# Modulation sums of block 1 placed earlier on VectorE, and a semaphore of its own for the second mixer's weights

## The chip, the cores and the metric

One NeuronCore of a Trainium2 chip runs the whole program in one launch. The metric is the device time of an execution in microseconds (us); less is better.

## What is computed

Two blocks of a transformer for one sequence of 256 tokens of width 1024, all in float32. The part that matters here is the start of block 1:

```python
mod = jax.nn.silu(c) @ ada_w[l] + ada_b[l]
sh_m, sc_m, g_m, sh_f, sc_f, g_f = jnp.split(mod, 6, axis=-1)
h = modulate(rms_norm(x, mix_norm_w[l]), sh_m, sc_m)
proj = h @ w_in[l]
y_r = rwkv7_group(proj[..., :RWKV_COLS], ...)
y_m = mlstm_group(proj[..., RWKV_COLS:], ...)
y = jnp.concatenate([y_r, y_m], axis=-1) @ w_out[l]
x = x + g_m[:, None, :] * y
```

`mod` is six vectors of 1024, each a product of `silu(c)` with a 1024x1024 piece of `ada_w`. The first two (shift and scale of the first norm) are needed before `proj`; the other four only after both mixers have begun. `proj` has 3336 columns: 13 chunks of 256 and eight gate columns. After block 1 come its mixture of experts and a second model of two layers with their own modulation, attention and MLPs.

## The kernel before

The program is written for the five engines by hand; semaphores order them. What it does in the first 200 us:

**The stream of weights.** SyncE (`block.sync`, L822 on) issues one list of 1 MB loads through a ring of eight buffers of 8 KB per partition. The list (L438 to 444) is `ada` 0 to 7, then in turn `win 7, ada 8, win 8, ada 9, win 9, ada 10, win 10, ada 11, win 11, ada 12, win 12, ada 13, win 0, ada 14, win 1, ada 15, ...`, `win 6, ada 20`, and last `ada` 21 to 23. Place i of the list goes to buffer i % 8, and its issue waits until place i - 8 has been used: a `win` chunk by TensorE, an `ada` piece by VectorE (`v_ada`). SyncE issues strictly in the order of the list. So `ada 14` (place 21) waits for the use of `ada 10` (place 13) and stands in the queue behind `win 0` (place 20).

**The modulation sums.** `ada_slot(n)` (L1560) on VectorE waits until piece n has landed and adds two products of 128x1024 to one of three sums (L1570 for the first product of a vector, L1572 for the others). Four pieces make a vector; where a piece opens the fourth, fifth or sixth vector (n = 12, 16, 20), it first waits for `t_ada`, TensorE's use of the sum that had been in the same place. VectorE takes its instructions strictly in the program's order: what stands behind an `ada_slot` that waits for its load, waits too.

**The chunks of `proj`.** `columns(n)` on TensorE makes 32 matmuls with chunk `win n` (L2245 or L2247). The order is 7, 8, the eight gate columns (`w.if`, L2261) and a small product for the attention bias of the second model (L2265), then 9, 10; transposes and broadcasts of the gate rows (`m.bc`, L2273 and L2275, behind `m.rows` of VectorE), `scores` 0 and 1 (L2252); chunk 11; then a wait for `m.z` of VectorE, `scores` 2 and 3, chunks 12 and 0; a wait for `m.pt` and the product of the second mixer (L2294, L2297); chunks 1 to 5, two of the modulation vectors (L2309, L600), chunk 6.

**The second mixer (mLSTM) on VectorE.** In order: gate bias (`w.gb`, L1612), the convolution (`m.conv`, L1630 and L1633), gate rows (`m.lf` of ScalarE awaited; L1639 to L1644), multiplication by the sigmoid of ScalarE (L1646; with it `m.rows` is reached), `m.z` (L1650 to L1654, behind `m.bc` of TensorE), `m.pt` (L1662 to L1666), and later the token shifts of the first mixer (`shift(n)`, L1619 and L1621). Between them stand the `ada_slot` calls.

**The bias write.** ScalarE sends, behind the gate rows, the attention bias of the second model to DRAM (L1316): 8 partitions are read 128 times each, 1.5 MB in rows of 1536 bytes, on ScalarE's own DMA queue (q10 in the profile; SyncE's is q1, GpSimd's q0).

**The small loads.** GpSimd issues them (L895 to L925). `gate_in` counts seven: two pieces of the gate columns, two gate biases, and the three small matrices `rwkv_w_up`, `rwkv_a_up` and `rwkv_g_up` of the first mixer. `hot_in` counts the two for the attention bias. VectorE (L1611) and TensorE (L2258) wait for all seven of `gate_in`; TensorE waits for `hot_in` ahead of L2265.

Of the kernel before, what the change touches and what calls it, by code (L numbers as in the profile page):

```python
# [114 lines left out]
def program(nc, A, out):  # L115
    ctx = ExitStack()
    with ctx:
        def sb(name, shape, dt=F32):
            return ctx.enter_context(nc.sbuf_tensor(name, shape, dt))

        def sem(name):
            return ctx.enter_context(nc.semaphore(name))
# [22 lines left out]
        def area(kb, words):  # L145
            return arena[:, int(kb * KB):int(kb * KB) + words]

        def area_r(kb, words):
# [49 lines left out]
        wup = sb("wup", [P, 2, 512])  # L198
        gup = area(47, 512)
# [13 lines left out]
        x_in, c_in, prm_in, col_in, par_in, gate_in, row_in = (  # L213
            sem(n) for n in ("x_in", "c_in", "prm_in", "col_in", "par_in", "gate_in", "row_in"))
# [94 lines left out]
        hots = arena[0:64, 30 * KB:30 * KB + 384]  # L309
        rel_sb = arena[0:64, 32 * KB:32 * KB + 8]  # L310
# [34 lines left out]
            sem(n) for n in ("t_gv", "a_gv", "t_gather", "t_gu", "t_turn", "t_dn", "t_scatter", "t_fin", "a_hg", "a_silu", "a_y", "v_sel", "v_act",  # L345
                             "v_hg", "v_turn", "v_ye", "v_ada2", "v_fin"))
        ring2 = [sem(f"ring2_{i}") for i in range(RING)]
        t_bin, t_bout, hot_in = (sem(n) for n in ("t_bin", "t_bout", "hot_in"))
        mlp_in = ring2
        ring2_n = [16 * len(range(i, 13, RING)) for i in range(RING)]  # L350
        t_up, t_ft, t_fd, a_fact, a_ft, v_fact_t, a_w1, v_w1, a_w2, v_w2 = (
# [100 lines left out]
        def loaded(eng, key):  # L452
            eng.wait_ge(ring_in[place[key] % RING], 16 * (place[key] // RING + 1))

        def slot(key):
            return ring[:, place[key] % RING, :]
# [411 lines left out]
        def _(pool):  # L868
# [46 lines left out]
            pool.dma_start(w_if[:, :, 32:36], w_in_t[:, :, 3332:3336]).then_inc(gate_in, 16)  # L915
            pool.dma_start(gate_b[0:4, 0:1], A["mlstm_i_b"].rearrange("o h -> h o")).then_inc(gate_in, 16)
            pool.dma_start(gate_b[32:36, 0:1], A["mlstm_f_b"].rearrange("o h -> h o")).then_inc(gate_in, 16)
            pool.dma_start(rel_sb[0:32, :], A["rel_bias_2"]).then_inc(hot_in, 16)
            pool.dma_start(hots[0:33, :], A["hots"]).then_inc(hot_in, 16)
            pool.wait_ge(v_ada, 16)  # L920
            pool.dma_start(wup[0:64, 0, :], A["rwkv_w_up"][0]).then_inc(gate_in, 16)
            pool.dma_start(wup[64:128, 1, :], A["rwkv_a_up"][0]).then_inc(gate_in, 16)
            pool.dma_start(gup[:, :], A["rwkv_g_up"][0]).then_inc(gate_in, 16)
            pool.dma_start(gate1[:, 0, :], A["ada_b"][:, 2 * D:3 * D].to_broadcast([P, D])).then_inc(par_in, 16)
            pool.dma_start(gate1[:, 1, :], A["ada_b"][:, 5 * D:6 * D].to_broadcast([P, D])).then_inc(par_in, 16)  # L925
            c = Counter(pool, g["c"], STEP["c.zeros"])
# [632 lines left out]
        def _(dve):  # L1559
            def ada_slot(n):  # L1560
                vec, q = n // 4, n % 4
                loaded(dve, ("ada", n))
                w = slot(("ada", n)).rearrange("p (t n) -> p t n", t=2)
                acc = macc[:, vec % 3, :]
                if q == 0 and vec >= 3:
                    dve.wait_ge(t_ada, vec - 2)
                for r in range(2):
                    k = 2 * q + r
                    if k == 0:
                        ins = nc.vector.tensor_scalar(acc, w[:, r, :], ccol[:, k:k + 1], None, ALU.mult)  # L1570
                    else:
                        ins = nc.vector.scalar_tensor_tensor(acc, w[:, r, :], ccol[:, k:k + 1], acc, ALU.mult, ALU.add)  # L1572
                    ada.link(ins)
# [30 lines left out]
            v_norm(dve, "n", mod_c[:, 0, :], mod_c[:, 1, :], mod_mix, meanwhile=lambda: ada_slot(6))  # L1604


            c = Counter(dve, v["w"])
            dve.wait_ge(t["w"], STEP["w.prm"])
            c.link(nc.vector.tensor_copy(prm_c[:, :], ps[:, 0, 256:408]))
            c.at("w.prmc")  # L1610
            dve.wait_ge(gate_in, 16 * 7)  # L1611
            c.link(nc.vector.tensor_scalar(gate_b[:, 1:2], gate_b[:, 0:1], 1 / CAP, None, ALU.mult))  # L1612
            c.at("w.gb")
            c.at("w.pre")
# [1 line left out]
            def shift(n):  # L1616
                dve.wait_ge(a["w"], STEP[f"w.col{n}"])
                dt = dtmp[:, :].rearrange("p (i t) -> p i t", i=2)
                c.link(nc.vector.tensor_tensor(dt, raw[:, n % 2, :, 0:256], raw[:, n % 2, :, 1:257], ALU.subtract))  # L1619
                for i in range(2):  # L1620
                    c.link(nc.vector.scalar_tensor_tensor(u[:, 2 * n + i, :], dt[:, i, :], mu_c[:, 2 * n + i:2 * n + i + 1],  # L1621
                                                          raw[:, n % 2, i, 1:257], ALU.mult, ALU.add))


            cm = Counter(dve, v["m"])
            ada_slot(8)
            ada_slot(9)
            for i in range(4):
                dve.wait_ge(a["w"], STEP[f"w.col{7 + i // 2}"])
                cm.link(nc.vector.tensor_scalar(qk[:, i, :], convraw[:, i, 3:259], cw_c[:, 12 + i:13 + i], cb_c[:, i:i + 1],  # L1630
# [3 lines left out]
                                                           cw_c[:, 4 * j + i:4 * j + i + 1], qk[:, i, :], ALU.mult, ALU.add))  # L1634
            cm.at("m.conv")

            dve.wait_ge(a["m"], STEP["m.lf"])
            one4 = ones2[0:4, :]
            cm.link(nc.vector.tensor_scalar(mrow[0:4, 0, :], mrow[0:4, 0, :], CAP, None, ALU.mult))  # L1639
# [2 lines left out]
            cm.link(nc.vector.tensor_tensor_scan(mrow[0:4, 5, :], one4, mrow[0:4, 4, :], 0.0, ALU.mult, ALU.max))  # L1642
            cm.link(nc.vector.tensor_tensor(mrow[32:36, 4, :], mrow[0:4, 2, :], mrow[0:4, 5, :], ALU.subtract))
            cm.link(nc.vector.tensor_copy(sel4[:, :, :], ident[0:4, 0:4].unsqueeze(2).to_broadcast([4, 4, P])))  # L1644
            dve.wait_ge(a["m"], STEP["m.sig"])
            cm.link(nc.vector.tensor_tensor(qk[:, :, :], qk[:, :, :], qsig[:, :, :], ALU.mult))  # L1646
            cm.at("m.rows")
            ada_slot(10)
            dve.wait_ge(t["m"], STEP["m.bc"])
            cm.link(nc.vector.tensor_copy(mcol[:, :, :], ps[:, 0, 0:128].rearrange("p (a n) -> p a n", a=2)))  # L1650
            for h in range(4):
# [2 lines left out]
                cm.link(nc.vector.tensor_scalar(mz[:, h, 256:384], mb[:, 128:256], mcol[:, 1, h:h + 1], 0.0,  # L1654
                                                ALU.subtract, ALU.max))
            cm.at("m.z")
            ada_slot(11)
            ada_slot(12)
            dve.wait_ge(a["m"], STEP["m.exp"])
            dve.wait_ge(g["c"], STEP["c.masks"])  # L1660
            cmask = m_causal.unsqueeze(1).to_broadcast([P, 4, P])
# [4 lines left out]
                cm.link(nc.vector.scalar_tensor_tensor(mz[:, h, :], ps[:, sc_bank[h], 0:384], 0.125, mz[:, h, :],  # L1666
                                                       ALU.mult, ALU.mult))
            cm.at("m.pt")
            ada_slot(13)
            ada_slot(14)  # L1670
            shift(0)
            dve.wait_ge(t["m"], STEP["m.num"])
            den, rec = small[:, 16:24], small[:, 24:32]
# [13 lines left out]
                                                AX_X, ALU.add))  # L1687
            cm.link(nc.vector.tensor_scalar(small[:, 8:16], small[:, 8:16], 1 / P, EPS, ALU.mult, ALU.add))
            cm.at("m.ss")
            ada_slot(15)  # L1690
            dve.wait_ge(g["m"], STEP["m.rs"])
            for tt in range(TT):
                yv = ym[:, tt, :].rearrange("p (h n) -> p h n", h=4)
# [2 lines left out]
            cm.at("m.s")  # L1696
            for n in range(1, 7):
                shift(n)
                ada_slot(15 + n)
            c.at("w.shift")  # L1700

            dve.wait_ge(t["w"], STEP["w.if"])
# [516 lines left out]
        def _(pe):  # L2219
# [15 lines left out]
            def columns(n):  # L2235
                i = win_order.index(n)
                loaded(pe, ("win", n))
                if i >= 2:
                    pe.wait_ge(a["w"], STEP[f"w.col{win_order[i - 2]}"])
                w = slot(("win", n)).rearrange("p (t n) -> p t n", t=8)  # L2240
                for j in range(2):
                    o = ps[:, 6 + i % 2, 256 * j:256 * j + 256]
                    for k in range(KT):
                        if n < 9:
                            ins = nc.tensor.matmul(o, w[:, k, P * j:P * j + P], hT[:, k, :], start=k == 0, stop=k == KT - 1)  # L2245
                        else:
                            ins = nc.tensor.matmul(o, hT[:, k, P * j:P * j + P], w[:, k, :], start=k == 0, stop=k == KT - 1)  # L2247
                ins.then_inc(t_win, 1)
# [6 lines left out]

            for n in (7, 8):
                columns(n)
            pe.wait_ge(gate_in, 16 * 7)  # L2258
            pe.wait_ge(v["w"], STEP["w.prmc"])
            for k in range(KT):  # L2260
                ins = nc.tensor.matmul(ps[0:36, 0, 0:256], w_if[:, k, :], hT[:, k, :], start=k == 0, stop=k == KT - 1)  # L2261
            c.mark(ins)
            c.at("w.if")
            pe.wait_ge(hot_in, 32)
            nc.tensor.matmul(ps[0:SWA_H, 4, 0:384], rel_sb[0:33, :], hots[0:33, :], start=True, stop=True).then_inc(t_bias, 1)  # L2265

            for n in (9, 10):
# [69 lines left out]

            c = Counter(pe, t["r"])
            pe.wait_ge(a["r"], STEP["r.u"])
            for tt in range(TT):  # L2340
                nc.tensor.matmul(ps[:, 4 + tt, :], u[:, 13, P * tt:P * tt + P], gup[:, :], start=True, stop=True)
            pe.wait_ge(v["r"], STEP["r.sq"])
# [299 lines left out]
            for i, (kind, _) in enumerate(ITEMS):  # L2642
                ahead = i < NI - 1 and "over" in (kind, ITEMS[i + 1][0])
                both_next = i % 2 and i < NI - 1
                if i == 0 or "over" not in (kind, ITEMS[i - 1][0]):
                    gate_up(i, 0)
                    gate_up(i, 1)
                if i:
                    scatter(i - 1)
                if both_next:  # L2650
                    gather(i // 2 + 1, 0)
                turn(i)
                if both_next:
                    gather(i // 2 + 1, 1)
                if i == 0:
                    gv_columns(3, ps[:, 5, 0:8])
                    gv_columns(4, ps[:, 5, 8:16]).then_inc(t_fin, 1)
                    for h in range(2):
                        gv_gate(2, h, h)
                    for h in range(2):  # L2660
                        gv_gate(5, h, 2 + h)
                if ahead:
                    gate_up(i + 1, 0)
                down(i)
                if ahead:
                    gate_up(i + 1, 1)
# [96 lines left out]
            for j in range(6):  # L2763
                hs = range(4 * j, 4 * j + 4) if j < 2 else range(2 * (j - 2), 2 * (j - 2) + 2)
                n = P if j < 2 else 2 * P
# [9 lines left out]
            for j in range(6):  # L2775
# [3 lines left out]
                for i in range(4):  # L2779
                    n = 4 * j + i  # L2780
# [100 lines left out]
```

## Time and profile before

| | us |
|---|---|
| median of 3 runs | 1256.24 |
| lowest and highest | 1245.6, 1258.23 |
| the profiled execution, its own time | 1254.31 |
| its span in the trace | 1252.6 |
| TensorE busy in the span | 1070.0 (85%) |
| VectorE busy | 640.0 (51%) |
| ScalarE busy | 351.5 (28%) |
| mean granted TensorE clock | 0.922 |

Times inside the trace count from the start of the span; the execution's own time is 1.7 us longer. A row of the timeline has the start, the duration, the engine, the line, the operation with what it writes and reads, how many stand in the row, and in square brackets the idle time before it and who ended it. SPq and ACTq are the instructions by which SyncE and ScalarE issue DMAs. "PEclk" is the granted clock of TensorE: 1.00 is 2.4 GHz, 0.50 is 1.2 GHz.

### The profile page before, as it was taken

The numbers are of one execution on the slowest core, as the hardware profiler recorded it, in microseconds if no ns is written. First come the engines' busy times: TensorE is split into PE (matmuls) and PEld (weight loads), VectorE is DVE, ScalarE is ACT, GpSimd is POOL, SyncE is SP. The second block draws the span as 40 slices with busy tenths as digits, with TensorE's granted clock in tenths as the row PEclk, the third lists the DMA queues.
The fourth block names the chain that finished last, engine by engine and source line by source line (L and its number), as shares of the span: only waits on it lengthen the run. The fifth ranks groups of instructions, "written<-read, shape, count | busy, mean of one in ns | idle before, by whom it ended". The sixth has DMA issues, their size and how long they took to land.

```text
span 1252.6 us, 16197 instructions
## 1 busy us (share of the span) xinstructions
PE 1070.0 (85%) x6588; PEld 814.6 (65%) x6588; DVE 640.0 (51%) x812; ACT 351.5 (28%) x440; POOL 178.0 (14%) x234
## 2 busy tenths in 40 slices
PE   1898977999978899999539794979999976999995
PEld 1787844997535455555227683858888865888884
DVE  6565567646444333323045727376757467553433
ACT  1130024241111111111023105166354315543531
POOL 4701013000200133231011004011111130000000
PEclk9998987999977999999869997889999977999998
DMA  9979638204679999999979703056676461545510
GB/s 352 351 163 307 242 123 305 102 1 169 228 305 408 383 401 353 356 339 355 407 226 371 277 1 135 1 203 251 235 294 225 134 247 73 192 144 194 225 67 34
DMA packets 114090, 287.48 MB, mean 230 GB/s; under 512 B 16406, under 2 KB 42334, under 8 KB 114026
## 3 DMA queue, kind: packets, MB, share of 16 engines
q1 hardware_dynamic: 94514, 245.45, 52.6%
q10 hardware_dynamic: 7560, 26.74, 6.3%
q0 software_dynamic: 11952, 14.38, 3.8%
q8 instruction: 46, 0.75, 0.2%
q14 instruction: 18, 0.15, 0.0%
HBM read 334.23 MB, written 2.62 MB: 269 GB/s over the span
## 4 chain that ended last, share of the span: by engine, by line
PE 68%; DMA 13%; DVE 10%; SPq 3%; ACT 2%; issue 2%; POOL 1%; DVEq 0%; ACTq 0%; POOLq 0%
PE ps L573 29%; PE ps L2245 6%; PE ps L2582 5%; DMA arena<-in_moe_w_down_dram 4%; PE ps L2561 4%; PE ps L2421 3%; DMA macc<-in_ada_w_dram 3%; PE ps L2609 3%; DMA ring<-in_w_in_dram 2%; PE ps L2508 2%; PE ps L2687 2%; SPq L763 1%; PE ps L2624 1%; DMA ring<-in_ada_w_dram 1%; SPq L619 1%
## 5 line engine op out<-in xcount | busy, mean ns | idle before, releaser
L578 DVE TENSOR_TENSOR ring_parts<-ring,arena_parts 128x2048 fp32r<-128x2048 f32 x65 | 146.6, 2286 | 49.1 <-ACT arena_parts L1109 42.1
L573 PE MATMUL ps<-arena_parts,macc_parts 128*128 128x512 f32 x512 | 166.0, 396 | 0.0
L573 PE MATMUL ps<-arena_parts,gate_parts 128*128 128x512 f32 x288 | 114.6, 398 | 8.3 <-DVE hT_parts L578 8.3
L573 PE MATMUL ps<-ring_parts,gate_parts 128*128 128x512 f32 x288 | 113.5, 394 | 0.0
L573 PE MATMUL ps<-arena_parts,hT_parts 128*128 128x512 f32 x288 | 113.4, 394 | 0.0
L573 PEld LDWEIGHTS ps<-arena_parts,macc_parts 128*128 128x128 f32 x512 | 96.2, 188 | 19.6
L573 PE MATMUL ps<-ring_parts,macc_parts 128*128 128x512 f32 x256 | 99.8, 390 | 0.0
L1109 ACT CAST arena_parts<-ring 128x2048 fp32r<-128x2048 f32 x32 | 60.3, 1908 | 84.5 <-DMA ring<-in_mlp_w_dram 43.4
L2245 PE MATMUL ps<-hT,ring 128*128 128x256 f32 x288 | 70.1, 409 | 5.6 <-DMA ring<-in_w_in_dram 5.6
L2245 PEld LDWEIGHTS ps<-hT,ring 128*128 128x128 f32 x288 | 59.5, 208 | 15.3 <-DMA ring<-in_w_in_dram 6.0
L573 PEld LDWEIGHTS ps<-arena_parts,gate_parts 128*128 128x128 f32 x288 | 55.1, 191 | 20.5 <-DVE hT_parts L578 9.1
L2582 PE MATMUL ps<-ring,hT 128*32 128x256 f32 x1024 | 61.7, 387 | 5.3 <-issue 3.4
L466 POOL TENSOR_TENSOR small<-small,nhalf 128x1 f32<-128x1 f32 x16 | 10.0, 625 | 390.1 <-DVE small L500 390.0
L573 PEld LDWEIGHTS ps<-arena_parts,hT_parts 128*128 128x128 f32 x288 | 55.0, 191 | 11.7
L573 PEld LDWEIGHTS ps<-ring_parts,gate_parts 128*128 128x128 f32 x288 | 55.1, 191 | 11.3
L1089 ACT CAST arena_parts<-ring 128x2048 fp32r<-128x2048 f32 x32 | 60.0, 1911 | 5.3 <-DMA ring<-in_mlp_w_dram 5.2
L578 DVE TENSOR_TENSOR macc_parts<-ps,macc_parts 128x512 fp32r<-128x512 f32 x32 | 22.1, 691 | 75.9 <-ACT macc_parts L1133 75.9
L2012 DVE SCALAR_TENSOR_TENSOR macc_parts<-ps,small,macc_parts 128x512 fp32r<-128x512 f32 x24 | 16.9, 747 | 85.8 <-ACT macc_parts L1439 85.8
L1572 DVE SCALAR_TENSOR_TENSOR macc<-ring,ccol,macc 128x1024 f32<-128x1024 f32 x42 | 54.0, 1285 | 8.5 <-DMA ring<-in_ada_w_dram 7.1
L2582 PEld LDWEIGHTS ps<-ring,hT 128*32 128x32 f32 x1024 | 34.3, 112 | 33.9 <-issue 13.5
L2609 PE MATMUL ps<-arena,gate 128*32 128x512 f32 x384 | 45.6, 607 | 10.8 <-DMA arena<-in_moe_w_down_dram 9.5
L573 PEld LDWEIGHTS ps<-ring_parts,macc_parts 128*128 128x128 f32 x256 | 48.2, 188 | 9.3
(539 smaller groups left out, 1799.0 us busy)
## 6 DMA issues: line engine op xcount, KB each, us to landing
ring<-in_mlp_w_dram SPq DMA_DIRECT2D x40, 1024.0 KB, 7.6
arena<-in_moe_w_down_dram SPq DMA_DIRECT2D x16, 2048.0 KB, 12.4
ring<-in_ada_w_dram SPq DMA_DIRECT2D x29, 1024.0 KB, 13.4
ring<-in_mlp_w_dram ACTq DMA_DIRECT2D x24, 1024.0 KB, 7.1
ring<-in_moe_w_up_dram SPq DMA_DIRECT2D x10, 2048.0 KB, 22.3
ring<-in_moe_w_gate_dram SPq DMA_DIRECT2D x10, 2048.0 KB, 17.8
arena<-in_ada_w_dram SPq DMA_DIRECT2D x15, 1024.0 KB, 7.0
ring<-in_w_in_dram SPq DMA_DIRECT2D x13, 1024.0 KB, 18.4
```

The source lines that it names most:

```text
L573: ins = nc.tensor.matmul(o, l, r, start=start and i == 0, stop=stop and i == 2, skip_group_check=True)
L578: return eng.tensor_tensor(lo, x, hi.bitcast(F32), ALU.subtract)
L1089: nc.scalar.copy(mlp_hi[s_], ring[:, s_, :]).then_inc(a_w2, 1)
L1109: nc.scalar.copy(mlp_hi[s_], ring[:, s_, :]).then_inc(a_w1, 1)
L1572: ins = nc.vector.scalar_tensor_tensor(acc, w[:, r, :], ccol[:, k:k + 1], acc, ALU.mult, ALU.add)
L2245: ins = nc.tensor.matmul(o, w[:, k, P * j:P * j + P], hT[:, k, :], start=k == 0, stop=k == KT - 1)
L2421: ins = nc.tensor.matmul(o, lhs[:, gi, hh], rhs[:, gi, hh], start=True, stop=True)
L2508: ins = nc.tensor.matmul(ps[:, 4 + j, :], hT[:, k, P * (j // 2):P * (j // 2) + P], w, start=k == 0, stop=k == KT - 1)
L2561: ins = nc.tensor.matmul(ps[:, 6 + i // 2, 256 * (i % 2):256 * (i % 2) + 256], xn[:, tt, P * k:P * k + P], picked[:, tt, :], start=tt == 0 ...
L2582: ins = nc.tensor.matmul(ps[rows, 4 + i % 2, FE * half:FE * half + FE], hT[:, k, P * (i % 2) + CAPQ * j:P * (i % 2) + CAPQ * j + CAPQ], w[ ...
L2609: ins = nc.tensor.matmul(ps[rows, 6 + h, :], tb[:, P * f + CAPQ * j:P * f + CAPQ * j + CAPQ], down_w[:, j, f, 512 * h:512 * h + 512], star ...
L2687: ins = nc.tensor.matmul(o, w[:, k, P * j:P * j + P], hT[:, k, :], start=k == 0, stop=k == KT - 1)
```

## The change

The calls of `ada_slot` move forward on VectorE, past the waits and past the mixer's work. The table shows what stands ahead of each step. No piece is added or dropped.

| ahead of | before | after |
|---|---|---|
| the copy of the parameters (L1609) | | 8, 9 |
| the convolution | 8, 9 | 10, 11 |
| the wait for `m.lf` | | 12 |
| the wait for `m.sig` | | 13 |
| the wait for `m.bc` (ahead of `m.z`) | 10 | 14 |
| the wait for `m.exp` (ahead of `m.pt`) | 11, 12 | 15 |
| `shift(0)` | 13, 14 | 16 |
| the wait for `m.rs` | 15 | 17 |
| behind `shift(1)` to `shift(6)` | 16 to 21, one each | 18 to 21, one each behind `shift(1)` to `shift(4)` |

The two loads of the attention bias now count on `gate_in` and the three small matrices on a semaphore of their own, `lora_in`; so `gate_in` is awaited at six. TensorE waits for `lora_in` ahead of the product with `gup` (L2341) and no longer for `hot_in`.

```diff
-            pool.dma_start(rel_sb[0:32, :], A["rel_bias_2"]).then_inc(hot_in, 16)
-            pool.dma_start(hots[0:33, :], A["hots"]).then_inc(hot_in, 16)
+            pool.dma_start(rel_sb[0:32, :], A["rel_bias_2"]).then_inc(gate_in, 16)
+            pool.dma_start(hots[0:33, :], A["hots"]).then_inc(gate_in, 16)
             pool.wait_ge(v_ada, 16)
-            pool.dma_start(wup[0:64, 0, :], A["rwkv_w_up"][0]).then_inc(gate_in, 16)
-            pool.dma_start(wup[64:128, 1, :], A["rwkv_a_up"][0]).then_inc(gate_in, 16)
-            pool.dma_start(gup[:, :], A["rwkv_g_up"][0]).then_inc(gate_in, 16)
+            pool.dma_start(wup[0:64, 0, :], A["rwkv_w_up"][0]).then_inc(lora_in, 16)
+            pool.dma_start(wup[64:128, 1, :], A["rwkv_a_up"][0]).then_inc(lora_in, 16)
+            pool.dma_start(gup[:, :], A["rwkv_g_up"][0]).then_inc(lora_in, 16)
...
+            ada_slot(8)
+            ada_slot(9)
             c = Counter(dve, v["w"])
             dve.wait_ge(t["w"], STEP["w.prm"])
             c.link(nc.vector.tensor_copy(prm_c[:, :], ps[:, 0, 256:408]))
             c.at("w.prmc")
-            dve.wait_ge(gate_in, 16 * 7)
+            dve.wait_ge(gate_in, 16 * 6)
...
             cm = Counter(dve, v["m"])
-            ada_slot(8)
-            ada_slot(9)
+            ada_slot(10)
+            ada_slot(11)
...
             cm.at("m.conv")
 
+            ada_slot(12)
             dve.wait_ge(a["m"], STEP["m.lf"])
...
+            ada_slot(13)
             dve.wait_ge(a["m"], STEP["m.sig"])
             cm.link(nc.vector.tensor_tensor(qk[:, :, :], qk[:, :, :], qsig[:, :, :], ALU.mult))
             cm.at("m.rows")
-            ada_slot(10)
+            ada_slot(14)
             dve.wait_ge(t["m"], STEP["m.bc"])
...
             cm.at("m.z")
-            ada_slot(11)
-            ada_slot(12)
+            ada_slot(15)
             dve.wait_ge(a["m"], STEP["m.exp"])
...
             cm.at("m.pt")
-            ada_slot(13)
-            ada_slot(14)
+            ada_slot(16)
             shift(0)
...
             cm.at("m.ss")
-            ada_slot(15)
+            ada_slot(17)
             dve.wait_ge(g["m"], STEP["m.rs"])
...
             for n in range(1, 7):
                 shift(n)
-                ada_slot(15 + n)
+                if n < 5:
+                    ada_slot(17 + n)
             c.at("w.shift")
...
-            pe.wait_ge(gate_in, 16 * 7)
+            pe.wait_ge(gate_in, 16 * 6)
...
-            pe.wait_ge(hot_in, 32)
...
             pe.wait_ge(a["r"], STEP["r.u"])
+            pe.wait_ge(lora_in, 16 * 3)
```

## Rows read from the trace of the kernel before

**Rows 1.** The page, part 4: shares of the chain that ended last, by engine

```profile
PE 68%; DMA 13%; DVE 10%; SPq 3%; ACT 2%; issue 2%; POOL 1%; DVEq 0%; ACTq 0%; POOLq 0%
```

**Rows 2.** The chain that ended last, in order of time: start us, us, what

```profile
68.67 30.57 DMA ring<-in_w_in_dram
99.28 9.43 PE ps L2245 x32
...
113.97 34.64 PE ps L2245 x160
148.61 1.72 PE ps L2309 x4
```

**Rows 3.** Timeline of TensorE, 38 to 240 us

```profile
75.48 0.33 PE L2273 MATMUL ps<-ident,arena 64*128 64x64 f32 x2
...
85.62 0.71 PE L2252 MATMUL ps<-arena 64*128 64x256 f32 x4
...
86.48 7.17 PE L2247 MATMUL ps<-ring,hT 128*128 128x256 f32 x32
99.28 9.43 PE L2245 MATMUL ps<-hT,ring 128*128 128x256 f32 x32 [5.62 <-DMA ring<-in_w_in_dram]
```

**Rows 4.** Busy time by engine in the stretch 99 to 102 us, then clock, DMA

```profile
99.00:102.00 3.00, 2.72 (x6) 2.18 (x7) 0.29 (x1) 0.00 (x0) 0.00 (x0) 0.50 1.00 350
```

**Rows 5.** Timeline of VectorE, 30 to 110 us and behind 110 us

```profile
49.34 0.15 DVE L1612 TENSOR_SCALAR gate_b<-gate_b 36x1 f32<-36x1 f32 x1 [8.08 <-DMA arena<-in_rwkv_g_up_dram]
...
54.39 0.41 DVE L1630 TENSOR_SCALAR arena<-arena,prm_c 128x256 f32<-128x256 f32 x1
...
60.87 1.53 DVE L1633 SCALAR_TENSOR_TENSOR arena<-arena,prm_c 128x256 f32<-128x256 f32 x3
65.53 0.28 DVE L1639 TENSOR_SCALAR arena<-arena 4x256 f32<-4x256 f32 x1 [3.14 <-ACT arena L1311]
...
68.17 0.41 DVE L1644 COPY arena<-ident 4x512 f32<-4x512 f32 x1
71.74 1.23 DVE L1646 TENSOR_TENSOR arena<-arena 128x1024 f32<-128x1024 f32 x1 [3.15 <-ACT arena L1321]
...
77.84 0.29 DVE L1650 COPY arena<-ps 128x128 f32<-128x128 f32 x1 [2.23 <-PE ps L2275]
...
81.40 0.35 DVE L1654 TENSOR_SCALAR arena<-ps,arena 128x128 f32<-128x128 f32 x1
...
101.71 2.61 DVE L1572 SCALAR_TENSOR_TENSOR macc<-ring,ccol,macc 128x1024 f32<-128x1024 f32 x2 [5.77 <-DMA ring<-in_ada_w_dram]
...
169.40 2.61 DVE L1572 SCALAR_TENSOR_TENSOR macc<-ring,ccol,macc 128x1024 f32<-128x1024 f32 x2
```

**Rows 6.** Timeline of SyncE's DMA issues, 0 to 240 us (`ada 11`, `ada 14`, `win 1`)

```profile
36.90 8.13 SPq L838 DMA_DIRECT2D ring<-in_ada_w_dram  x1
...
75.63 0.37 SPq L838 DMA_DIRECT2D ring<-in_ada_w_dram  x1
76.04 7.53 SPq L841 DMA_DIRECT2D ring<-in_w_in_dram  x1
```

**Rows 7.** Line L838, the one issue at 36.9 us (`ada 11`)

```profile
DMA to landing us min/median/max: 21.4/21.4/21.4
```

**Rows 8.** Line L838, the one issue at 75.6 us (`ada 14`)

```profile
DMA to landing us min/median/max: 26.0/26.0/26.0
```

**Rows 9.** Timeline of ScalarE: the issue of the bias write

```profile
65.96 1.28 ACTq L1316 DMA_DIRECT2D bias_rows<-arena  x1
```

**Rows 10.** DMA queues, 68 to 70 us: packets, MB, share of 16 engines

```profile
q10 hardware_dynamic: 70, 0.11, 45.4%
q1 hardware_dynamic: 8, 0.02, 3.0%
```

**Rows 11.** DMA queues, 88 to 98 us

```profile
q10 hardware_dynamic: 326, 0.50, 41.8%
q1 hardware_dynamic: 334, 0.34, 9.6%
```

More of the change, by code:

```diff
@@ L347, in program @@
         ring2 = [sem(f"ring2_{i}") for i in range(RING)]
-        t_bin, t_bout, hot_in = (sem(n) for n in ("t_bin", "t_bout", "hot_in"))
+        t_bin, t_bout, lora_in = (sem(n) for n in ("t_bin", "t_bout", "lora_in"))
         mlp_in = ring2
```

## The prediction

> **What bounds the kernel now.** I read the page first: its chain of work that ended last is 68% TensorE, 13% DMA and 10% VectorE [rows 1]. So an edit on VectorE counts only where TensorE waits for VectorE, or where it moves a load. I then read that chain in order of time for the first 200 us, where all edits lie [rows 2]. TensorE works through the chunks of `proj` without a pause up to 93.65 us (86.48 + 7.17, [rows 3]); then it stands 5.62 us for chunk `win 0`, whose load took 30.57 us. After that nothing holds it until it has finished its first modulation vector behind chunk 5: chunk 0 from 99.28, the product of the second mixer, chunks 1 to 5 in 34.64 us, that is 6.93 us a chunk. Chunk 0 itself took 9.43 us. The granted clock at its start was 0.50, 1.2 GHz, after the pause [rows 4]; the pause has cost 9.43 - 6.93 = 2.5 us in clock besides its 5.62.
>
> Why did `win 0` need 30.57 us? The views of the queues and the timelines say it. ScalarE issues the bias write at 65.96 [rows 9]. From then on its queue q10 holds some 45% of the 16 engines, as many as eight of them busy nearly all the time [rows 10]. At 68 to 70 us SyncE's queue q1 is almost empty (8 packets): everything issued ahead of `win 0`, so `ada 13` too, is through. And late in the write, from 88 to 98 us, q1 gets 334 packets of about 1 KB through against 326 of q10 [rows 11]: one for one, on the engines that the write holds, 33 a microsecond, where the free engines stand idle. Rows of 1 KB are those of a `win` chunk. So half of `win 0` crawls beside the bias write, and lands when the write ends, near 99 us. `ada 14`, issued at 75.63 behind it [rows 6], lands 26.0 us later [rows 8], at 101.6; in the kernel before VectorE asks for it at about 96 and waits 5.77 us, up to 101.71 [rows 5]. That wait costs nothing there, since `shift(0)` behind it has to wait for chunk 0 until 109 us anyway.
>
> **The change, part by part.**
>
> The semaphores. VectorE stood 8.08 us at the gate bias for the last of the small matrices [rows 5]; this wait is shorter now. But nothing behind it is late in the kernel before: the convolution begins at 54.39 and TensorE needs its result only through ScalarE's sigmoid, after 68 us. The matrices land before 49.34 and TensorE first needs them behind 170 us, so the new wait for `lora_in` costs 0. The bias loads are issued ahead of the matrices and are waited for behind chunk 8, at 57 us: 0. GpSimd's order of issues doesn't change.
>
> Pieces 8 to 13. One piece costs 2.61 us [rows 5]. 8 and 9 have been issued long before and fill the idle time ahead of 49 us. Piece 11 is now waited for ahead of the convolution: it lands at 36.90 + 21.4 = 58.3 [rows 6, 7]. Its issue stays where it is (its buffer was free long before). So VectorE: piece 11 to 60.9, the convolution (8.0 us, from 54.39 to 62.40 before, [rows 5]) to 69.0, piece 12 to 71.6, gate rows (3.05 us, 65.53 to 68.58) to 74.7, piece 13 to 77.3, the multiplication (1.23) to 78.6. ScalarE's sigmoid began at about 69.3 before, so it isn't held by a convolution that ends at 69.0. TensorE wants the gate rows at 75.48 [rows 3] and so is 3.1 us late here. This is not yet a loss at the end, as 5.62 us of idle time lie ahead of chunk 0.
>
> Piece 14. It now stands ahead of the wait for `m.bc`, and so ahead of `m.z`; before, piece 10 stood there, landed long ago. SyncE can issue 14 sooner: its buffer (piece 10) is free by about 52 us, so it follows `win 0` at about 69.3 instead of 75.63. But on the engines that the bias write holds it stands behind the half of `win 0` that crawls. I take it that it lands where it did, at 101.6, because the row shows that q1 moves nothing else there until the write ends. Then VectorE sits from 78.6 to 101.7 on a load. Queued behind it on VectorE are `m.z`, `m.pt` and the shifts; behind `m.z` on TensorE `scores` 2 and 3, chunk 12 and chunk 0. In numbers: piece 14 ends at 101.71 + 2.61 = 104.3; the `m.z` group takes 3.9 us (77.84 to 81.75, [rows 5]), to 108.3. TensorE, which reached this point at 85.62, takes 8.03 us for `scores` and chunk 12 (85.62 to 93.65, [rows 3]) to 116.3, and then chunk 0. It has stood idle for about 20 us, so it pays the low clock once, as before: I use the same 9.43 us for chunk 0, and the end is at 125.8 against 108.71. **The loss is 17.05 us.** The low clock is the unsure part: none of it would make it 14.5, twice of it 19.6; I take once, since the one pause of this stretch in the trace cost 2.5.
>
> After chunk 0. `m.pt` needs VectorE's 15 and some 4 us behind ScalarE's exponential, so it is ready near 115, ahead of 125.8. Chunks 1 to 5 run as before, 17 us later; their loads have 17 us more. Pieces 15 to 19 have landed when VectorE comes to them. Piece 20 opens the sixth vector and must wait until TensorE has used the third sum (L2309, at 148.61 before, [rows 2], now near 166): VectorE stands there with shifts 4 and 5 behind it. After it lie 20, 21 and two shifts, about 8 us, to 174, and chunk 6 comes only at 183.9. Hidden by chunk 6; without that cover it would cost 8 us.
>
> The tail. Behind `shift(6)` piece 21 (169.40, 2.61 us, [rows 5]) stood ahead of VectorE's work for the first mixer, on the chain. It is gone from there: **a gain of 2.6 us**, kept as long as VectorE sets the pace, which it does up to the POOL products near 193 us.
>
> **The sum:** + 17.05 - 2.6 = + 14.4 us. Against the profiled execution's own time (span 1252.6, 1.7 us around it): 1254.3 + 14.4 = 1268.7, I say 1269. The median of the runs shown is 1.9 us above that execution, so the same difference would make it 1270.6 there.
>
> The Trainium skill, "DMA: Bandwidth & Descriptors", section on queues, rings and completion order, says that on each DMA engine the descriptors of one queue are taken in ring order. By that rule `ada 14` can't pass `win 0` however early it is issued, and the sum stands; the trace agrees, with 99.2 and 101.6 us for two loads that were issued 7 us apart. The same page (why a DMA increments its semaphore by 16) lets a transfer of eight rows run on eight engines only; the 45% of q10 agrees.
>
> **The rivals.**
>
> B, the load is hidden anyway: `ada 14`, issued at 69.3, is in by the time VectorE asks for it. For it: half the engines were free from 74 us. Against it: the write holds the other half to 98. Then `m.rows` at 78.6, piece 14 to 81.2, `m.z` at 85.1; TensorE comes there at 85.62 + 3.1 = 88.7, ends chunk 12 at 96.8, waits 2.5 us for `win 0`, and does chunk 0 in 9.43 or, the pause being shorter, in 6.93. With the tail that is - 2.6 to - 5.1: 1251.7 to 1249.2, not slower than before. It decides for B if `ada 14` lands before about 82.
>
> C, the landing follows the issue: 26.0 us behind 69.3 is 95.3, 6.3 us sooner. Then + 17.05 - 6.3 - 2.6 = + 8.1: 1262.4. For it speaks only that the issue moves. By the Trainium skill's ring order, C could not be. I leave it a chance, as this trace has no piece issued so close behind a crawling chunk.
>
> D, a real gain: `win 0` too comes at once and the pause at 93.65 closes, - 5.6 - 2.5 - 2.6 = - 10.7: 1243.6. Nothing in the edit moves the bias write or the issue of `win 0` (it waits for chunk 9 on TensorE at 68.66).
>
> **How the numbers follow.** The forecast (A) 0.74, C 0.12, B 0.12, D 0.02. The bounds of A, from the low clock, are 1266.2 and 1271.2; with the spread of the runs (8.7 below and 3.9 above the profiled execution) A reaches from 1262 to 1275. Taking in C and leaving out B and D, the range is 1258 to 1275. A measurement of this kernel can tell about 1%, some 12.5 us, from no change. A lies above that by only 2 us: of its 0.74 I give 0.57 to slower by over 1% and 0.17 to within 1%; B and C are within 1%. D falls short of 1% even at its full size, so faster by over 1% gets 0.03.
>
> **What the changed profile would show.** VectorE idle for some 20 us up to about 101.7, ended by a DMA into `ring`, right ahead of L1572 and L1650. TensorE idle from about 88.7 to 108.3, ended by VectorE's L1654, where before there were 5.62 us for `win 0`. The bias write issued near 66 and `win 0` landed near 99 as before. L1572 gone from behind the last `shift`, and L1703 right behind L1621. If TensorE's long pause is missing, B holds; if it ends near 102, C. I would be wrong altogether if the bias write were issued at another time, for all the landings hang on it.

## The result, and the profile after

The changed kernel takes 1265.38 us (median of 18 runs, 1259.55 to 1273.15) against 1255.79 us before (18 runs, 1245.6 to 1260.66) on the same chips: a ratio of 1.0094, 95% interval 1.0072 to 1.0115. Slower, by 9.0 to 14.4 us of 1255.79. (The two medians differ by 9.6 us; the ratio with its interval is what I go by, here and below.) The profiled execution has a span of 1262.8 us against 1252.6.

The page of the changed kernel, part 4, against [rows 1]. DMA into `ring` from `ada_w` has risen from 1% of the span to 6%. Two pieces are new: 21.18 us up to the landing of piece 11, and 32.95 us up to that of piece 14, which is in the second fence.

```profile
PE 67%; DMA 13%; DVE 11%; SPq 3%; ACT 2%; issue 2%; POOL 1%; DVEq 0%; ACTq 0%; POOLq 0%
PE ps L573 29%; DMA ring<-in_ada_w_dram 6%; PE ps L2585 5%; PE ps L2248 4%; PE ps L2564 4%; PE ps L2424 3%; DMA arena<-in_moe_w_down_dram 3%; DMA macc<-in_ada_w_dram 3%; PE ps L2612 3%; PE ps L2511 2%; PE ps L2690 2%; PE ps L2627 2%; SPq L763 1%; DVE macc L1572 1%; SPq L619 1%
```

The chain that ended last, changed kernel, 60 to 195 us (start us, us, what), against [rows 2]:

```profile
69.03 32.95 DMA ring<-in_ada_w_dram
102.08 1.30 DVE macc L1572
...
108.69 1.23 PE ps L2255 x4
...
110.34 8.92 PE ps L2250 x32
119.27 6.91 PE ps L2248 x32
...
131.42 34.64 PE ps L2248 x160
```

Before, the load on the chain at this place was `win 0`, and TensorE waited for it. Now it is `ada 14`; VectorE waits for it, and TensorE for VectorE.

VectorE's timeline, changed kernel, against [rows 5]:

```profile
44.97 0.15 DVE L1614 TENSOR_SCALAR gate_b<-gate_b 36x1 f32<-36x1 f32 x1 [0.22 <-DMA arena<-in_hots_dram]
...
58.17 2.60 DVE L1572 SCALAR_TENSOR_TENSOR macc<-ring,ccol,macc 128x1024 f32<-128x1024 f32 x2 [5.35 <-DMA ring<-in_ada_w_dram]
...
76.69 1.22 DVE L1650 TENSOR_TENSOR arena<-arena 128x1024 f32<-128x1024 f32 x1
102.08 2.61 DVE L1572 SCALAR_TENSOR_TENSOR macc<-ring,ccol,macc 128x1024 f32<-128x1024 f32 x2 [24.16 <-DMA ring<-in_ada_w_dram]
...
108.28 0.35 DVE L1658 TENSOR_SCALAR arena<-ps,arena 128x128 f32<-128x128 f32 x1
...
167.92 0.76 DVE L1570 TENSOR_SCALAR macc<-ring,ccol 128x1024 f32<-128x1024 f32 x1 [13.16 <-PE ps L2311]
```

The gate bias is 4.4 us earlier and waits for nothing to speak of. Piece 11 is waited for at 58.17, ahead of the convolution. Then comes the row of this case: 24.16 us idle in front of piece 14. The last row is piece 20, which waits 13.16 us for TensorE's use of the third sum.

TensorE's timeline, changed kernel, against [rows 3]:

```profile
77.97 0.34 PE L2275 MATMUL ps<-ident,arena 64*128 64x64 f32 x2 [2.66 <-DVE arena L1650]
...
81.98 9.48 PE L2250 MATMUL ps<-ring,hT 128*128 128x256 f32 x32
108.69 1.23 PE L2255 MATMUL ps<-arena 64*128 64x256 f32 x4 [17.23 <-DVE arena L1658]
...
110.27 8.99 PE L2250 MATMUL ps<-ring,hT 128*128 128x256 f32 x32
119.10 7.07 PE L2248 MATMUL ps<-hT,ring 128*128 128x256 f32 x32
```

Two waits for VectorE that weren't there before: 2.66 us for the gate rows and 17.23 us for `m.z`. The 5.62 us for `win 0` are gone.

SyncE's issues, changed kernel, against [rows 6] (`win 0`, `ada 14`, `win 1`):

```profile
68.44 0.55 SPq L841 DMA_DIRECT2D ring<-in_w_in_dram  x1
69.03 4.62 SPq L838 DMA_DIRECT2D ring<-in_ada_w_dram  x1
...
75.34 8.32 SPq L841 DMA_DIRECT2D ring<-in_w_in_dram  x1
```

and the landing of the issue at 69.0, against [rows 8]:

```profile
DMA to landing us min/median/max: 33.0/33.0/33.0
```

`ada 14` is issued 6.6 us earlier (69.03 against 75.63) and lands at 102.0 against 101.6. The queues from 88 to 98 us, against [rows 11], share the engines in the same way:

```profile
q10 hardware_dynamic: 322, 0.49, 41.8%
q1 hardware_dynamic: 336, 0.34, 9.7%
```

### The profile page after: what moved, and what is told of

Read it like the earlier page. It is cut to its first block, busy times and chain, and to the rows that moved or that the text cites. A ratio compares the mean times of both kernels' runs of the same rounds, so it can differ in the third digit from the quotient of the medians.

```text
span 1262.8 us, 16198 instructions
## 1 busy us (share of the span) xinstructions
PE 1067.8 (85%) x6588; PEld 813.2 (64%) x6588; DVE 638.7 (51%) x812; ACT 351.7 (28%) x440; POOL 176.4 (14%) x234
## 4 chain that ended last, share of the span: by engine, by line
PE 67%; DMA 13%; DVE 11%; SPq 3%; ACT 2%; issue 2%; POOL 1%; DVEq 0%; ACTq 0%; POOLq 0%
PE ps L573 29%; DMA ring<-in_ada_w_dram 6%; PE ps L2585 5%; PE ps L2248 4%; PE ps L2564 4%; PE ps L2424 3%; DMA arena<-in_moe_w_down_dram 3%; DMA macc<-in_ada_w_dram 3%; PE ps L2612 3%; PE ps L2511 2%; PE ps L2690 2%; PE ps L2627 2%; SPq L763 1%; DVE macc L1572 1%; SPq L619 1%
```

## The experiments

To read them, it helps to have a mark at which the whole stretch is over: the first matmuls of the first mixer's chunk products (L2412 in the kernel before, 217.73 us; a row of 32). The table has, from each kernel's profile, the start of this row, the span, and what is left of the span behind the mark. The ratios are to runs of the kernel before on the same chips.

| kernel | mark, us | against before | span | behind the mark | ratio, 95% interval |
|---|---|---|---|---|---|
| before | 217.73 | | 1252.6 | 1034.9 | |
| the change | 231.29 | + 13.6 | 1262.8 | 1031.5 | 1.0094 [1.0072, 1.0115] |
| the change, again | 231.59 | + 13.9 | 1266.7 | 1035.1 | one execution, 1268.4 us |
| semaphores alone | 216.53 | - 1.2 | 1258.2 | 1041.7 | 0.9997 [0.9962, 1.0031] |
| sums 14 and 15 late | 213.56 | - 4.2 | 1255.1 | 1041.5 | 0.9987 [0.9955, 1.0019] |
| sum 21 alone | 214.76 | - 3.0 | 1252.5 | 1037.7 | 0.9973 [0.9941, 1.0006] |
| change, bias write late | 214.97 | - 2.8 | 1242.9 | 1027.9 | 0.9991 [0.9956, 1.0026] |
| before, sum 21, bias write late | 205.65 | - 12.1 | 1234.4 | 1028.8 | 0.9914 [0.9876, 0.9951] |
| change, ada 14 ahead of win 0 | 219.57 | + 1.8 | 1254.7 | 1035.1 | 1.0054 [1.0017, 1.0091] |
| change, half the bias write | 219.02 | + 1.3 | 1248.2 | 1029.2 | 1.0000 [0.9963, 1.0036] |

What is left behind the mark varies by 14 us among executions of the same code there (1027.9 to 1041.7). The three smallest are those of the three versions with the bias write late, whole or in part. That is no proof of a gain there: the profiled execution of the changed kernel with the late write (1244.64 us) lay 7.3 us below the median of its 12 runs (1251.93). So single spans say little about effects of some us. The mark too comes from one execution of each kernel, and differences of 1 to 2 us in it are not to be read: in the two executions of the changed kernel, the same program, chunk 9 already began at 61.23 and at 59.94. The ratios over many runs decide.

### The semaphores alone

The kernel before with the lines on `gate_in`, `hot_in` and `lora_in`, no sum moved.

> The kernel before with only the semaphores of the change (gate_in awaited at six, lora_in of its own); no modulation sum is moved. My theory: the shorter wait at the gate bias is followed by nothing that is late, so 0 us against the kernel before, ratio within 0.998 to 1.002. Rival (the new wait for the first mixer's matrices costs, or the earlier gate bias gains): 1 us or more either way, seen at the product with gup or at the convolution.

Measured: ratio 0.9997 (0.9962 to 1.0031). The gate bias ran at 44.63, 4.7 us earlier than [rows 5], and at the mark TensorE was 1.2 us ahead, of which 0.6 were there at 75 us already (74.9 against 75.48). Nothing late stood behind that wait. What VectorE gained at the gate bias it spent in waits for ScalarE inside the convolution (0.90 and 2.81 us), and the product with `gup` waits for ScalarE as before (3.52 us), not for `lora_in`. The part is worth nothing that could be measured.

### Sums 14 and 15 behind m.pt

```diff
             cm.at("m.rows")
-            ada_slot(14)
             dve.wait_ge(t["m"], STEP["m.bc"])
...
             cm.at("m.z")
-            ada_slot(15)
...
             cm.at("m.pt")
-            ada_slot(16)
+            for n in (14, 15, 16):
+                ada_slot(n)
             shift(0)
```

> The changed kernel with only sums 14 and 15 put behind m.pt (so 14, 15, 16 stand ahead of shift(0)). My theory, that the loss is VectorE standing ahead of m.z on piece 14: the stall of 24 us is gone from TensorE's path, chunk 0 begins when win 0 lands (99.3) and the kernel is some 5 us faster than before (- 2 at chunk 0 as the pause gets short, - 3 to - 4 at the tail): 1249 to 1253. Rival, that the earlier sums 11 to 13 (gate rows 2.5 us late, chunk 11 at the low clock) make the loss: it stays near 1265.

VectorE's timeline:

```profile
102.85 2.61 DVE L1572 SCALAR_TENSOR_TENSOR macc<-ring,ccol,macc 128x1024 f32<-128x1024 f32 x2 [3.83 <-DMA ring<-in_ada_w_dram]
108.34 2.60 DVE L1572 SCALAR_TENSOR_TENSOR macc<-ring,ccol,macc 128x1024 f32<-128x1024 f32 x2 [2.89 <-DMA ring<-in_ada_w_dram]
```

and TensorE's:

```profile
77.92 0.34 PE L2274 MATMUL ps<-ident,arena 64*128 64x64 f32 x2 [2.56 <-DVE arena L1650]
...
100.39 7.17 PE L2247 MATMUL ps<-hT,ring 128*128 128x256 f32 x32 [1.01 <-DMA ring<-in_w_in_dram]
```

Piece 14 lands as late as ever (VectorE begins it at 102.85), but nothing that TensorE needs stands behind it. The stall is gone, chunk 0 begins at 100.39, and the mark is 4.2 us ahead of the kernel before; the ratio is 0.9987 (0.9955 to 1.0019), which is no gain clear of nothing; the 5 us expected lie just within the interval. The rival falls: sums 11 to 13 stand where the change put them and the gate rows are as late (2.56 us), yet the loss isn't there. So the places of 14 and 15, which this edit moved together, make the whole of it. The trace of the changed kernel says which: `m.z`, for which TensorE stood 17.23 us, stands behind 14 and ahead of 15. Sum 14 alone was not moved.

### Sum 21 alone

```diff
             for n in range(1, 7):
                 shift(n)
-                ada_slot(15 + n)
+                if n < 6:
+                    ada_slot(15 + n)
+                if n == 5:
+                    ada_slot(21)
```

> The kernel before with the semaphores of the change and one sum moved alone: 21 stands behind shift(5) with 20 and no longer behind shift(6). My theory: the tail is worth 2.6 us by the sum's duration; in the changed kernel it was 3.9, so 2.6 to 4 us faster than before, ratio 0.997 to 0.998. Rival: the gain is taken back by work after it, 0 us.

Ratio 0.9973 (0.9941 to 1.0006), the mark 3.0 us ahead although `win 0` landed 1.2 us later in this execution (chunk 0 began at 100.45). VectorE needed 4.6 us from the end of the last shift to the end of the modulation vectors, where it was 8.3 before: 3.7 less, the same as in the changed kernel. The timed ratio by itself is not clear of nothing. Its VectorE rows behind the last shift:

```profile
168.92 1.01 DVE L1621 SCALAR_TENSOR_TENSOR arena<-dtmp,prm_c,arena 128x256 f32<-128x256 f32 x2
169.96 0.29 DVE L1706 COPY early<-ccol 128x256 f32<-128x256 f32 x1
```

### The bias write late

The changed kernel, but ScalarE issues the bias write behind the copy of chunk 4, near 142 us.

```diff
-            act.dma_start(scratch_d..., ebc...).then_inc(bias_out, 16)
             columns(9)
...
             for n in range(7):
                 columns(n)
+                if n == 4:
+                    act.dma_start(scratch_d..., ebc...).then_inc(bias_out, 16)
...
-            dve.wait_ge(bias_out, 16)
...
-            pool.wait_ge(bias_out, 16)
             pool.wait_ge(v["m"], STEP["m.s"])
             c.link(nc.gpsimd.memset(bhz[:, :, :], 0.0))
+            pool.wait_ge(bias_out, 16)
```

> The changed kernel with the bias write of ScalarE issued behind chunk 4's copy (near 142 us) and not at 66; VectorE no longer waits for it, GpSimd waits for it behind its first memset. My theory, that the bias write holds half the engines and so piece 14: win 0 lands near 75 and ada 14 near 78, VectorE stands at most 2 us on it, chunk 0 ends near 106 and the kernel is about 6 us faster than before, near 1250. Rival, that ada 14 is late for its place behind win 0 and the traffic of SyncE's own queue: it still lands near 100 and the time stays near 1265. A third outcome: the write, now beside the loads of ada 20 to 23 and those of the second model's sums, makes a wait there; then a wait of TensorE at L2325 for ring or arena appears near 180 us.

VectorE's timeline, piece 13 (not in the fence), the multiplication, piece 14:

```profile
76.92 1.22 DVE L1651 TENSOR_TENSOR arena<-arena 128x1024 f32<-128x1024 f32 x1
78.18 2.61 DVE L1573 SCALAR_TENSOR_TENSOR macc<-ring,ccol,macc 128x1024 f32<-128x1024 f32 x2
```

and TensorE's:

```profile
78.20 0.47 PE L2275 MATMUL ps<-ident,arena 64*128 64x64 f32 x2 [4.28 <-DVE arena L1651]
...
100.52 7.07 PE L2248 MATMUL ps<-hT,ring 128*128 128x256 f32 x32
```

Every sum stands where the change put it, and piece 14 is there when VectorE comes to it: no idle time at all. `win 0` landed 5.3 us behind its issue, at 72.4, and `ada 14` 7.2 us behind its own, at 74.9. The loads were late only by the bias write. Chunk 0 ended at 107.6, 1.6 us later than expected, since TensorE now paid 4.28 us for the late gate rows, ran at the low clock behind this pause (chunk 11 took 8.83 us), and had no wait for `win 0` to hide either in. The third outcome did not come: no wait for a load near 180 us, and the one at 206 took 2.30 us (1.93 in the kernel before). The timed gain wasn't clear of nothing (0.9991, 0.9956 to 1.0026), and the 6 us expected lie outside the interval; the mark is 2.8 us ahead. So taking the write away removes the loss, and no more is shown.

### Before with sum 21 and the late bias write

The kernel before with the semaphores, with the two edits just shown, and no other sum moved.

> The kernel before with the semaphores, with sum 21 behind shift(5), and with the bias write issued behind chunk 4's copy. All other sums stand where they stood before, so the gate rows are in time. My theory: win 0 lands near 75, TensorE goes from chunk 12 to chunk 0 without a pause at 93.6 and ends it near 100.6 (before 108.7), and the tail gives 3.7: by the end of the stretch 11 to 12 us ahead of the kernel before, near 1243. Rival, that the pause is only moved (win 1 or 2 late, or the write beside the loads of the second model's sums costs): a new wait of TensorE behind 100 us, and less than 6 us gained.

The chain in order of time:

```profile
85.84 7.10 PE ps L2250 x32
92.94 6.91 PE ps L2248 x32
...
105.10 34.64 PE ps L2248 x160
```

Ratio 0.9914 (0.9876 to 0.9951), that is 6.1 to 15.5 us less (medians: 1239.33 us of 7 runs against 1253.9 of 24), and the mark 12.1 us ahead, as reckoned. Chunk 0 follows chunk 12 without a pause and at the full clock (6.91 against 9.43 in [rows 2]). This version beats both kernels. TensorE has four waits for the second model's loads behind 190 us, of 0.2 to 1.6 us each and 4.3 us together, where the kernel before has one of 1.93; they are small beside the gain.

### ada 14 ahead of win 0 in the list

```diff
             for i, n in enumerate(win_order):
-                stream += [("win", n)] + [("ada", 8 + i)]
+                stream += [("ada", 8 + i), ("win", n)] if n == 0 else [("win", n), ("ada", 8 + i)]
```

> The changed kernel with one swap in SyncE's list: ada 14 is issued ahead of win 0. My theory (the write keeps its engines to itself until about 83, then shares them packet by packet, and each engine takes SyncE's loads in the order of issue): ada 14 lands near 88 and not at 102, VectorE's idle time ahead of it falls from 24 us to about 10, TensorE's from 17 to about 4; win 0 lands near 100 all the same; ratio to the kernel before near 1.000. Rival (the landing of ada 14 doesn't hang on what stands ahead of it, only on the end of the write): it lands at 99 or later, ratio 1.009 as the changed kernel.

VectorE's timeline, pieces 14 and 15:

```profile
87.94 2.60 DVE L1572 SCALAR_TENSOR_TENSOR macc<-ring,ccol,macc 128x1024 f32<-128x1024 f32 x2 [9.62 <-DMA ring<-in_ada_w_dram]
...
106.03 2.61 DVE L1572 SCALAR_TENSOR_TENSOR macc<-ring,ccol,macc 128x1024 f32<-128x1024 f32 x2 [11.54 <-DMA ring<-in_ada_w_dram]
```

`ada 14` is in at 87.9, at the time expected, while `win 0`, now behind it, lands at 100.4 and the bias write lasts to between 99 and 100 us as before. So the place in SyncE's queue decides when a load comes through beside the write, and the rival (only the write's end counts) falls. The time expected was wrong: ratio 1.0054 (1.0017 to 1.0091), where 1.000 was expected. I had not followed piece 15, which now stands ahead of `m.exp` and waits 11.54 us; it delays `m.pt` past the end of chunk 0 (1.34 us on TensorE). That explains the mark (+ 1.8), not all of the ratio; the rest stays open.

### Half the bias write

The changed kernel with 64 of the 128 rows of each partition at the old place, and the others behind chunk 4's copy (`bias_out` is awaited at 32).

> The changed kernel with the bias write cut in two: 64 of the 128 rows of each partition at the old place, the other 64 behind chunk 4's copy. My theory: the first part keeps eight engines to itself for some 16 us, to about 83; then win 0's second half needs 1 to 2 us at full speed and ada 14 lands near 86 to 88. VectorE's idle time ahead of piece 14 falls from 24 us to about 9; ratio to the kernel before near 1.000. Rival (the share of engines doesn't matter, the loads of SyncE's queue fill the time): ada 14 lands beyond 95.

```profile
88.88 2.60 DVE L1575 SCALAR_TENSOR_TENSOR macc<-ring,ccol,macc 128x1024 f32<-128x1024 f32 x2 [10.72 <-DMA ring<-in_ada_w_dram]
```

Half the write, and VectorE's idle time falls from 24.16 to 10.72 us (about 9 had been expected); the ratio is 1.0000 (0.9963 to 1.0036). Whole, half and none of the write at this place give piece 14 at 102.1, 88.9 and (at the latest) 78.2.

### The change again

> The changed kernel as it is, a second look. In its first profile TensorE was 13.5 us late at the end of the mixers' preparation (216.7 us before, 230.3 after) and the span only 10.2 us longer. My theory: the difference behind that point is the chance of an execution (at which points TensorE's clock falls), so the start of that point repeats within 1 us of 230.3 and the remainder of the span differs by some us from 1032.5. Rival: the change gives back 3 us later on, and then the remainder is 1032 to 1033 again.

The mark fell at 231.59 against 231.29, and 1035.1 us were left behind it against 1031.5. The 3.4 us by which the first span looked better than the mark did not come again, which speaks for the chance of an execution and against the rival. One execution does not rule the rival out: the timed runs give + 11.8 us where the marks give + 13.6 and + 13.9, and the interval (9.0 to 14.4) holds both. The marks agree better than the stretch ahead of them: in the second execution chunk 0 began 1.8 us earlier (117.30 against 119.10), and TensorE lost this again between 210 and 231 us, at the low clock and in a longer wait for a load (3.61 against 2.42 us). The mean granted clock was 0.914 in the first execution and 0.906 in the second; which way the clock and the time hang together was not tried.

## Why the prediction was right

The time (1265.38) lies in the range, and the forecast case, A, is what the trace shows. Point by point:

**The semaphores, 0.** Right, by the experiment with them alone.

**Pieces 8 to 13.** Reckoned: piece 11 from 58.3, gate rows and multiplication done at 78.6, TensorE 3.1 us late. Measured: 58.17, 77.9, and 2.66 us. What I missed: the short wait too was followed by a low clock, and chunk 11 took 9.48 us and not 7.17. It cost nothing, as TensorE then had to wait for `m.z` anyway (hence 17.23 us of idle time where I had about 19.6). With the stall gone it costs: in the changed kernel with the late bias write chunk 0 ends at 107.6, in the version with the old places of these sums at 99.9. Of these 7.7 us the gate rows' lateness is 3.4 (78.20 against 74.76), and the rest is the low clock behind the pause. So a lateness of some 3 us costs more than twice as much where nothing hides it, and the prediction had no term for the clock behind it.

**Piece 14.** Reckoned: it lands at 101.6 in spite of its earlier issue, `m.z` is ready at 108.3, chunk 0 ends at 125.8. Measured: 102.0, 108.6, 126.2 by the chain. The same 17.4 us for `scores`, chunk 12 and chunk 0 came out, with the low clock in chunk 12 (8.99 us) and chunk 0 at full speed (7.07). Of the rivals, B (hidden anyway) and C (the landing follows the issue) asked for idle times of VectorE that end before 82 and at 95; it ended at 102.08. The rule of the Trainium skill that I named ("DMA: Bandwidth & Descriptors", queues, rings and completion order: one queue's descriptors are taken in ring order on each engine) was put to the test by the swap: by it `ada 14` must come out first when it is issued first, and it came out 14 us sooner, ahead of `win 0` at 100.4.

**Piece 20.** Reckoned to stand up to 166 and to be hidden by chunk 6. It stood until 167.92, and the last of the two shifts and sums ended at 176.2 where chunk 6 came at 184.1.

**The tail, - 2.6.** Mis-sized: from the end of the last shift to the end of the modulation vectors VectorE took 3.7 us less. The sum is 2.6 of it. The other 1.1 is the copy behind it, which the prediction had left at its old time. Changed kernel:

```profile
185.55 1.01 DVE L1623 SCALAR_TENSOR_TENSOR arena<-dtmp,prm_c,arena 128x256 f32<-128x256 f32 x2
186.59 0.29 DVE L1706 COPY early<-ccol 128x256 f32<-128x256 f32 x1
```

and the kernel before, VectorE's and GpSimd's timelines at the same place:

```profile
172.04 1.40 DVE L1703 COPY early<-ccol 128x256 f32<-128x256 f32 x1
```

```profile
171.49 1.80 POOL L972 MEMSET arena<- 128x2048 f32 x1
```

The same copy takes 1.40 us while a memset of GpSimd runs, and 0.29 when it begins ahead of the memsets. It took 1.40 with the semaphores alone and 0.29 wherever sum 21 was moved. GpSimd's memsets are released by the last shift (the first begins at 169.47, 0.1 us behind it), and sum 21 stood between that shift and the copy. In the kernel before the copy ends 0.15 us behind the memset, as if it had waited for it; that the memset is the cause is read from these rows, and no run separates it.

**The sum.** + 14.4 was forecast for the stretch. At the mark the two executions show + 13.6 and + 13.9. In the first, chunk 0 ends 17.5 us later than before where 17.05 were forecast, and the tail gives 3.7 where 2.6 were; the two misses together make 0.7 of the 0.8 us between forecast and mark. The ratio over 18 runs gives + 11.8 us, 9.0 to 14.4, so the forecast stands at its upper end. Of the 2.6 us between, the tail explains 1.1; the rest is not resolved. The point value, 1269, is 3.6 us above the median of 1265.38. Setting out from one execution of 1254.3 made it look better than it was: on the median of the 18 runs before (1255.79) the same sum gives 1270.2, 4.8 us too high. The median also lies a little below the bounds that I gave case A for the low clock alone (1266.2 to 1271.2), though the low clock cost what I had reckoned.

**The chances.** I gave 0.57 to slower by over 1% and less to within 1%. The measured 0.94% (0.72 to 1.15) lies within, and the interval does not decide between the two. The chances by size also add up to more than 1: 0.57 and 0.03, and 0.17, 0.12, 0.12 and D's 0.02 for within 1%. And the 1262 at the lower end of A does not follow from its terms: 1266.2 - 8.7 is 1257.5.

## What to carry to other kernels

Moving work ahead of a wait on an engine that works in order moves the waits inside that work too: for each step moved, look up when its load lands, not when its buffer is free, and ask who stands behind it. A load lands late where it shares DMA engines with a long transfer that holds a few of them, though the two are on different queues; that transfer, and not the consumer's place, is then the thing to move, as the version with the late bias write shows. A gain at the end of a stretch (sum 21) and a loss in its middle (sum 14) came in one edit; only apart do they show what each is worth. And a small lateness that hides behind another wait is not free: it comes out, with the low clock behind its pause, when that wait is taken away.

## What the runs showed of the hardware

A write that reads 8 partitions, on ScalarE's queue, kept SyncE's packets off the engines that it used until about halfway through (from 67 to about 83 us, of some 33 us), and only then let them in one for one. With half of the write, `win 0` and `ada 14` landed at 86.2 and 88.8 us, and in the changed kernel at 99.2 and 102.0. I had read the sharing from the second half (334 against 326 packets) and had not expected the first half to be closed. In the kernel before, no packet of q1 was seen from 74 to 76 us, when `win 0` was not through; this is the only row of that stretch:

```profile
q10 hardware_dynamic: 68, 0.10, 45.9%
```

In the changed kernel none was seen from 78 to 82 us, when both `win 0` and `ada 14` had been issued and had not landed. The Trainium skill ("DMA: Bandwidth & Descriptors", queues, rings and completion order) says that an engine drains a whole packet of one queue, typically 9 to 17 descriptors and at most 64, before it turns to the next. With 128 rows per engine a packet of 64 would fit the closed first half; it does not fit the second half, where the two queues go one for one, and no run here separates it from other causes.

A pause of TensorE of only 2.66 us was followed by the low clock. In the changed kernel TensorE stood from 75.3 to 78.0 and then took up the gate rows' transposes and broadcasts; the granted clock was still 0.98 from 77 to 80 us and then fell to the lower level, 1.2 GHz (the stretch, the busy times by engine, and behind them the clock):

```profile
80.00:84.00 4.00, 4.00 (x15) 2.86 (x14) 0.00 (x0) 0.00 (x0) 0.00 (x0) 0.50 0.47 58
84.00:87.00 3.00, 3.00 (x10) 2.41 (x9) 0.00 (x0) 0.00 (x0) 0.00 (x0) 0.55 0.91 195
```

All six profiled executions with a pause at this place (2.56 to 4.33 us) show it, with 7.95 to 9.48 us for chunk 11; the four without the pause took 7.17 us for the same matmuls.
